# The second mixer of a two-block transformer on one NeuronCore: delta rule by pairs of heads beside the projections

## The chip, the cores and the metric

The kernel runs on one core of a Trainium2 chip. The metric is the device time in microseconds (us) of one execution, as the median of several runs. The trace is one further execution of the same program.

## The reference, cut to what matters

The program is two transformer blocks; all arithmetic is float32. The second block's first mixer works on 512 tokens: 256 of a context stream and 256 of a latent stream. Its input projection has parts `a_u`, `a_v` (a gated MLP), `qkv` and `gate` (a gated delta rule with 4 heads of 128, in both directions), and the decays and betas.

```python
def chunk_gmlp(u, v, ln_g, ln_b, ws, bs):
    u = gelu(u);  v = layer_norm(gelu(v), ln_g, ln_b)
    s = einsum('gij,bnjgd->bnigd', ws, chunks_of_128(v)) + bs
    return u * s

def gdn_chunked(q, k, v, g, beta, s0):        # per head, per chunk
    gcum = cumsum(g);  decay = exp(gcum_i - gcum_j) on and below the diagonal
    a_mat = strict_lower((k * beta) @ k.T * decay)
    t_mat = inverse(eye + a_mat)
    u = t_mat @ (v * beta);  w = t_mat @ (k * beta * exp(gcum))
    attn = (q @ k.T) * decay
    # over chunks, in order:
    v_new = u - w @ s
    o = (q * exp(gcum)) @ s + attn @ v_new
    s = s * exp(gcum_end) + (k * exp(gcum_end - gcum)).T @ v_new

def gated_deltanet(...):
    hq = silu(dwconv(qkv, conv_w));  q, k, v = split(hq);  q, k = l2norm(q), l2norm(k)
    o = forward scan + flipped backward scan
    return rms_norm(o, norm_g) * silu(gate)
y = concatenate([chunk_gmlp, gated_deltanet]) @ w_out
```

The context pass hands its final state to the latent pass. After `w_out` each stream gets a gated residual and a convolutional feed-forward.

## The kernel before, in words

All weights come as 547 tiles of 1 MB through a ring of 7 buffers (`load_turns`, line 166), in the order in which the program uses them; the host packs the stream in that order. `tile_used` counts used tiles and lets the next load start. A tile of a feature projection is 128 x 8 x 256: two halves of 128 features, each 8 products of 128x128 by 128x512, into one PSUM bank of 8 (`feature_tile`, line 198). One float32 product shows as two MATMUL records. `token_rows` (line 213) makes the rows of `v`: 2 tiles, 32 products in all.

Each engine runs its own instructions in program order. Semaphore counts (`Done`) order the engines. `after_all(eng)` makes an engine wait for all that the current chain has issued. `side_by_side` takes a list of generators and advances each by one `yield` in turn: one such turn is called a round here. It fixes the program order of every engine's queue; it doesn't look at times. TensorE needs no wait for its own earlier work.

The mixer has four stages.

1. `first_units` (line 1763) multiplies the first two tiles of the stream, which are those of `u`; `token_rows` follows with `v` in banks 0 to 3, then GELU on ScalarE.
2. `side_by_side` over three convolution lanes (`conv_lane`, line 1924; q, k and v, two of six tiles each, with products, taps, SiLU, square sums, root and transposes), a small lane (`gate_lane`: 2 tiles, w_ab; then `decay_steps`, `spatial_steps`), and `layer_norm_lane`.
3. A memset of the output sum on GpSimd (line 2135), and then `side_by_side` over four `delta_pair(d, pair)` chains: two directions by two pairs of heads. A chain has two PSUM banks of its own, starts `STAGGER * lane` rounds late (STAGGER is 5), and goes over 4 chunks of 128 tokens. A chunk has 35 yields: 7 for decays and triangular parts (ScalarE at 2182, TensorE at 2193 to 2196, VectorE at 2204, ScalarE at 2213, VectorE at 2223 to 2233, TensorE at 2241 and 2245), 20 for five levels of the inverse (TensorE 2281, ScalarE 2289, TensorE 2311 and 2314, VectorE 2322 to 2327), and 8 for the rest (TensorE 2337, 2352, 2369, 2385 to 2387, the others between). At 2213 stand the Exp functions.
4. The tail, in one stretch over all 16 head and tile pairs: squares on ScalarE (2415), power on GpSimd, scaling (2433), 16 transposes (2442), gating (2452). After it `modulation` (lines 996 and 997), and `out_stage`, whose products read the result `yT` (line 352) and whose gate diagonals are made at line 333.

```python
        def side_by_side(chains):
            before = {d: d.n for d in everyone}
            running = [(g, dict(before)) for g in chains]
            while running:
                for g, own in list(running):
                    chain.append(own)
                    if next(g, "end") == "end":
                        running.remove((g, own))
                    chain.pop()
```

Of the kernel before, what the change touches and what calls it, by code (L numbers as in the profile page):

```python
# [19 lines left out]
P = 128  # L20
# [43 lines left out]
def build(nc, stream, params, where, out):  # L64
# [4 lines left out]
    with ExitStack() as ctx:  # L69
# [245 lines left out]
        def out_stage(src, ktiles, ntt, x, outs_of, diag, gate=None, hidden_ready=None, kept=None, last_rows=None):  # L315
# [7 lines left out]
            if gate:  # L323
                layer, which, streams, rows, scr = gate
                groups = [(st, q) for st in streams for q in range(2)]
                gate_banks = range(4) if ntt == 4 else range(2)

                @block.vector
                def _(dve):
                    after_all(dve)  # L330
                    for n, (st, q) in enumerate(groups):
                        col = 24 * which + 16 + 4 * q
                        last = nc.vector.tensor_tensor(
                            scr[:, n, :].rearrange("p (a b) -> p a b", a=4), ident.unsqueeze(1).to_broadcast([P, 4, P]),
                            ada[:, layer, col:col + 4, st].unsqueeze(2).to_broadcast([P, 4, P]), ALU.mult)
                    dve_done.by(last)
                diag_known = dve_done.n

            def products(n, t, first):
                b = down[n][t]  # L340

                @block.tensor
                def _(pe):
                    claim(pe, b)
# [15 lines left out]
            def gate_rows_now():  # L360
                @block.tensor
                def _(pe):
                    pe.wait_ge(dve_done.sem, diag_known)
                    for n, b in zip(range(len(groups)), gate_banks):
                        claim(pe, b)
                        last = nc.tensor.matmul(ps[:, b, :], ones, scr[:, n, :], start=True, stop=True)  # L366
# [3 lines left out]
                def _(act):  # L370
                    act.wait_ge(pe_done.sem, pe_done.n)
# [5 lines left out]
            def add(n, t, summed, rows_known):  # L377
# [3 lines left out]
                def _(dve):  # L381
                    wait_marks(dve, [summed])
                    if gate:
                        dve.wait_ge(act_done.sem, rows_known)
                        st = streams[0] if ntt == 2 else (1, 1, 0, 0)[t]
                        link(dve, dve_done, nc.vector.tensor_tensor(scr[:, t, :], ps[:, b, :],  # L386
                                                                    rows[:, st, n * 512:n * 512 + 512], ALU.mult))
                        dve_done.by(nc.vector.tensor_tensor(xs, xs, scr[:, t, :], ALU.add))
# [1383 lines left out]
        def _(pe):  # L1772
            claim(pe, 4, 5, 6, 7)
            for n in range(2):
                t = tile_used.n + n
                pe.wait_ge(landed[t % RING], 16 * (t // RING + 1))
                first_units(pe, n, slice(0, SEQ))
# [20 lines left out]

        def gate_buffers():
            return take(2, D), take(4, 512)  # L1800

        reset(4 * 512)
# [4 lines left out]
        for i in range(4):  # L1807
            @block.scalar
            def _(act):
                act.wait_ge(tile_used.sem, tile_used.n - 1 + i // 2)  # L1810
                act_done.by(nc.scalar.activation(uT[:, i, :], ps[:, 4 + i, :], ACT.Gelu))
                freed[4 + i] = [(act_done, act_done.n)]
        token_rows([0, 1, 2, 3], hT, 0, KT)
        for t in range(T4):
            @block.scalar
            def _(act):
                act.wait_ge(tile_used.sem, tile_used.n)
                act_done.by(nc.scalar.activation(vn[:, t, :], ps[:, t, :], ACT.Gelu,
                                                 accum_out=small[:, 8 + t:9 + t]))
                freed[t] = [(act_done, act_done.n)]  # L1820

# [3 lines left out]
        mark_gdn = cur[0]  # L1825
        scratch512 = take(512)
        cbs = [take(2, 512) for _ in range(3)]
# [3 lines left out]
        def layer_norm_lane():  # L1831

            @block.vector
            def _(dve):
                after_all(dve)
                link(dve, dve_done, nc.vector.tensor_scalar(small[:, 12:16], small[:, 8:12], 1.0 / 512, None,
                                                            ALU.mult))
                for t in range(T4):
                    last = nc.vector.tensor_scalar(vn[:, t, :], vn[:, t, :], small[:, 12 + t:13 + t],
                                                   None, ALU.subtract)  # L1840
                dve_done.by(last)
# [3 lines left out]
            def _(act):  # L1845
                after_all(act)
                for t in range(T4):
                    link(act, act_done, nc.scalar.activation(scratch512, vn[:, t, :], ACT.Square,
                                                             accum_out=small[:, 8 + t:9 + t]))
            yield  # L1850
            rstd_of((8, 12), 512)
            yield

            @block.vector
            def _(dve):
                after_all(dve)
                for t in range(T4):
                    last = nc.vector.scalar_tensor_tensor(vn[:, t, :], vn[:, t, :], small[:, 24 + t:25 + t],
                                                          c("ln_g"), ALU.mult, ALU.mult)
                link(dve, dve_done, last)  # L1860
            yield

            @block.vector
            def _(dve):
                for t in range(T4):
                    last = nc.vector.tensor_tensor(vn[:, t, :], vn[:, t, :], c("ln_b"), ALU.add)
# [1269 lines left out]
```

## Time and profile before

| what | us |
|---|---|
| median of three runs | 3143.01 |
| lowest and highest run | 3138.71, 3143.89 |
| time of the profiled execution | 3139.56 |
| its span | 3137.6 |
| TensorE busy, of the span | 2915.2 (93%) |
| VectorE busy | 624.6 (20%) |
| ScalarE busy | 396.7 (13%) |
| mean granted TensorE clock | 0.960 |

The span runs from the first to the last instruction. The mixer lies between 1660 and 2160 us. TensorE's busy time there has to be read with the granted clock beside it, since a record takes twice as long on the lower level, and the record of a short matmul includes the time in which the next one has already begun.

### The profile page before, as it was taken

The page shows a single profiled execution, that of the slowest core. Times are in us where ns is not written, and L with a number is a line of the kernel's source. Part 1 is how long each engine was busy: PE and PEld are TensorE (multiplying, and loading weights), DVE is VectorE, ACT ScalarE, POOL GpSimd, SP SyncE. Part 2 cuts the span into 40 slices and gives each one's busy share as a digit, 9 for nine tenths or more (in the row PEclk, how much of TensorE's full clock was granted, in tenths as well). Part 3 has the DMA queues.
Part 4 walks back from the last instruction along what each step waited for, and adds up shares of the span by engine and source line. Part 5 has one row for each costly group of instructions (what it writes and reads, how often), then busy time and mean ns, then how long its engine had stood idle before and what let it go on. Part 6 is the DMA issues. An engine that isn't in the chain of part 4 may idle for free. (4 is left out here: it accounts for less than half of the span.)

```text
span 3137.6 us, 70498 instructions
## 1 busy us (share of the span) xinstructions
PE 2915.2 (93%) x31472; PEld 2178.4 (69%) x31472; DVE 624.6 (20%) x1701; ACT 396.7 (13%) x1066; POOL 32.7 (1%) x46
## 2 busy tenths in 40 slices
PE   5889999999999999999999996887999999889999
PEld 2567856679989899999996465774544444545883
DVE  0121001121100000001001135663222210223331
ACT  1110001110000000000001123332111100122210
POOL 0000000000000000000000000000000000000000
PEclk9899999999999999999999987888999999999999
DMA  8783434259989899999992110000112202311442
GB/s 346 303 333 134 149 146 147 106 213 347 365 339 369 337 369 351 365 364 358 357 385 91 67 41 15 2 2 25 70 67 81 81 27 81 134 67 54 144 151 80
DMA packets 80495, 585.60 MB, mean 187 GB/s; under 512 B 8912, under 2 KB 8912, under 8 KB 10064
## 3 DMA queue, kind: packets, MB, share of 16 engines
q1 hardware_dynamic: 79920, 580.15, 48.6%
q8 instruction: 251, 4.11, 0.5%
q10 hardware_dynamic: 288, 1.05, 0.1%
q14 instruction: 36, 0.29, 0.0%
HBM read 580.11 MB, written 1.05 MB: 185 GB/s over the span
## 5 line engine op out<-in xcount | busy, mean ns | idle before, releaser
L1448 PE MATMUL ps<-arena,ring 128*64 128x96 f32 x14336 | 601.9, 246 | 9.3 <-issue 8.1
L1448 PEld LDWEIGHTS ps<-arena,ring 128*64 128x64 f32 x14336 | 594.5, 137 | 20.3 <-issue 18.5
L2500 PE MATMUL ps<-hT,ring 128*128 128x256 f32 (+2 forms) x1472 | 455.3, 472 | 5.6 <-ACT hT L464 3.4
L2500 PEld LDWEIGHTS ps<-hT,ring 128*128 128x128 f32 x1472 | 274.5, 190 | 185.2 <-issue 166.3
L352 PE MATMUL ps<-ring,arena 128*128 128x512 f32 x896 | 388.3, 594 | 4.4 <-DVE small L996 4.4
L352 PEld LDWEIGHTS ps<-ring,arena 128*128 128x128 f32 x896 | 170.4, 191 | 216.4 <-issue 214.9
L1482 PE MATMUL ps<-arena,ring 128*64 128x96 f32 x7168 | 302.7, 246 | 10.2 <-issue 9.3
L1482 PEld LDWEIGHTS ps<-arena,ring 128*64 128x64 f32 x7168 | 297.8, 137 | 14.4 <-issue 13.4
L198 PE MATMUL ps<-hT,ring 128*128 128x256 f32 (+1 forms) x608 | 192.9, 478 | 8.2 <-ACT arena L749 4.0
L198 PEld LDWEIGHTS ps<-hT,ring 128*128 128x128 f32 x608 | 117.2, 194 | 81.8 <-issue 72.3
L1520 DVE TENSOR_TENSOR arena<-arena,ps 128x96 f32<-128x96 f32 x224 | 57.0, 255 | 574.2 <-ACT arena L1498 574.2
L1498 ACT ACTIVATE arena<-ps 128x96 f32<-128x96 f32 x224 | 56.3, 251 | 882.8 <-PE ps L1448 882.8
L923 PE MATMUL ps<-hT,ring 128*128 128x256 f32 (+1 forms) x736 | 152.7, 370 | 2.6 <-ACT hT L462 2.6
L923 PEld LDWEIGHTS ps<-hT,ring 128*128 128x128 f32 x736 | 134.8, 190 | 20.3 <-issue 3.0
L2545 DVE SCALAR_TENSOR_TENSOR arena<-ps,par,arena 128x510 f32<-128x510 f32 (+1 forms) x88 | 50.1, 611 | 300.6 <-ACT arena L2533 300.6
L213 PE MATMUL ps<-ring,hT 128*128 128x512 f32 (+1 forms) x224 | 96.5, 590 | 0.0
L568 PE MATMUL ps<-ring,arena 128*32 128x256 f32 x768 | 53.0, 437 | 35.9 <-DMA ring<-in_stream 35.9
L2533 ACT ACTIVATE arena<-ps,par 128x512 f32<-128x512 f32 (+1 forms) x88 | 46.3, 577 | 278.6 <-PE ps L2500 278.6
L213 PEld LDWEIGHTS ps<-ring,hT 128*128 128x128 f32 x224 | 43.2, 194 | 51.3 <-issue 47.1
L386 DVE TENSOR_TENSOR arena<-ps,arena 128x512 f32<-128x512 f32 x24 | 16.6, 692 | 261.2 <-PE ps L352 210.6
L1551 DVE COPY arena<-ps 128x384 f32<-128x384 f32 x16 | 8.9, 558 | 299.4 <-PE ps L1482 299.4
L568 PEld LDWEIGHTS ps<-ring,arena 128*32 128x32 f32 x768 | 28.5, 125 | 55.0 <-issue 44.2
(508 smaller groups left out, 2267.9 us busy)
## 6 DMA issues: line engine op xcount, KB each, us to landing
ring<-in_stream SPq DMA_DIRECT2D x547, 1024.0 KB, 6.0
par<-in_params SPq DMA_DIRECT2D x1, 3397.0 KB, 28.7
h<-in_x ACTq DMA_DIRECT2D x2, 512.0 KB, 7.8
cx<-in_ctx SPq DMA_DIRECT2D x2, 512.0 KB, 29.5
out<-h SPq DMA_DIRECT2D x4, 256.0 KB, 2.0
par<-in_params SPq DMA_DIRECT2D x1, 941.0 KB, 6.0
```

The source lines that it names most:

```text
L198: last = nc.tensor.matmul(o[:, 0:ntok], w[:, k, half * P:half * P + P], src[:, k, tok0:tok0 + ntok], start=(k == 0), stop=(k == KT - 1))
L213: last = nc.tensor.matmul(ps[:, b, 0:cols], src[:, k, tok0 + n * P:tok0 + n * P + P], w[:, k - t0, 0:cols], start=(k == 0), stop=(k == kti ...
L352: last = nc.tensor.matmul(ps[:, b, :], src[:, k, t * P:t * P + P], w[:, k % kper, :], start=(k == 0), stop=(k == ktiles - 1))
L568: last = nc.tensor.matmul(ps[32 * j:32 * j + 32, 7, 0:256], cond[:, k, :], w, start=(k == 0), stop=(k == KT - 1))
L923: last = nc.tensor.matmul(ps[:, b, half * SEQ + tok.start:half * SEQ + tok.stop], w[:, k, half * P:half * P + P], hT[:, k, tok], start=(k ...
L1448: last = nc.tensor.matmul(ps[m:m + 64, 4 + s % 2, half * P:half * P + CAP], w[:, k, half * P + m:half * P + m + 64], hTe[:, k, :], start=( ...
L1482: last = nc.tensor.matmul(ps[m:m + 64, 6 + half, q * P:q * P + CAP], w[:, j, q * P + m:q * P + m + 64], hid[:, 4 * d + j, :], start=(d == ...
L1498: nc.scalar.activation(sg[:, s % 2, :], ps[:, 4 + s % 2, 0:CAP], ACT.Silu).then_inc(moe_silu, 1)
L1520: nc.vector.tensor_tensor(hid[:, s, :], sg[:, s % 2, :], ps[:, 4 + s % 2, P:P + CAP], ALU.mult).then_inc(moe_hid, 1)
L2500: last = nc.tensor.matmul(ps[:, 2 * BANKS_CONV[f % RING] + half, tok], w[:, k, half * P:half * P + P], hT[:, k, tok], start=(k == 0), stop ...
L2533: nc.scalar.activation(buf[:, b, :], ps[:, 2 * b + half, 0:ntok], ACT.Copy, scale=tap(1, half, f)).then_inc(conv_centre, 1)
L2545: nc.vector.scalar_tensor_tensor(seg(o, 1, SEQ), seg(x, 0, SEQ - 1), tap(0, half, f), seg(o, 1, SEQ), ALU.mult, ALU.add).then_inc(conv_lef ...
```

## The change

The four stages become one `side_by_side` over decay lane, two delta lanes, projections, three convolution lanes, the MLP's rows and four tail quarters:

```diff
-        side_by_side([conv_lane(0), conv_lane(1), conv_lane(2), small_lane(), layer_norm_lane()])
-        side_by_side([delta_pair(d, pair) for d in range(2) for pair in range(2)])
+        side_by_side([decay_lane(), delta_lane(0), delta_lane(1), projections(),
+                      conv_lane((2, 3, 1), (4, 5), gT[:, 0:2, :]), conv_lane((4, 5), (6, 7), gT[:, 2:4, :]),
+                      conv_lane((0,), (0, 1), vn[:, 0:2, :]), mixed_rows(),
+                      *(tail_steps(pair, half) for pair in range(2) for half in range(2))])
```

`first_units` now takes tiles 2 and 4 of qkv (k and v of the first two heads). The stream order follows the order of use. `projections` issues the other products one by one:

```diff
+        def between(n):
+            for _ in range(2 if deltas else n % 2):
+                yield
+        def tile_products(kind, banks):
...
+            for half in range(2):
+                while banks[half] in busy:
+                    yield
+                for k in range(KT):
...                 # one product; weights(pe, kind) at the first
+                    if k < KT - 1 or half == 0:
+                        yield from between(k)
+        def value_rows():
+            while busy & {4, 5, 6, 7} or 0 not in conv_done:
+                yield
...                 # 2 halves x 4 row tiles x 4 products, each with: yield from between(k)
+        def projections():
+            used[0] = (yield from tile_products("qkv0", (0, 1)))[1][1]
+            for banks, n in (((3, 2), 0), ((6, 7), 2)):
+                halves = yield from tile_products("u", banks)
+                evacuated(halves, banks, [uT[:, n + i, :] for i in range(2)], ACT.Gelu)
+            for n, banks in ((3, (4, 5)), (5, (6, 7)), (1, (4, 5))):
+                used[n] = (yield from tile_products(f"qkv{n}", banks))[1][1]
+                yield
+            yield from value_rows()
+            while not {1, 3, 5} <= set(conv_done):
+                yield
+            for banks, n in (((4, 5), 0), ((6, 7), 2)):
+                halves = yield from tile_products("out_gate", banks)
+                evacuated(halves, banks, [gT[:, n + i, :] for i in range(2)], ACT.Silu, ...)
+            gates_of.extend(marks_here())
```

A delta lane takes one direction and does its two pairs of heads one after the other, 4 chunks of 35 yields each. The body of a chunk is that of before, except that the first chunk reads no state and the last writes none:

```diff
-        def delta_pair(d, pair):
-            for _ in range(STAGGER * lane):
-                yield
-            for T in ((0, 1, 2, 3), (1, 0, 3, 2))[d]:
+        def delta_lane(d):
+            for pair in range(2):
+                needed = (0, 2, 4) if pair == 0 else (1, 3, 5)
+                while not set(needed) <= set(conv_done) or not decays:
+                    yield
+                if pair == 0:
+                    while busy & {ba, bb}:
+                        yield
...
+                    for _ in range(STAGGER * d):
+                        yield
+                    deltas.append(d)
+                for step, T in enumerate(((0, 1, 2, 3), (1, 0, 3, 2))[d]):
...
+                    lane_marks[d, pair].append(marks_here())
+                    yield
```

`decay_lane` is `decay_steps` with the start of the small lane: 8 yields, in bank 2. `conv_lane(todo, bank, cb)` does `conv_steps(n, ...)` for each n once its tile is multiplied: 11 yields for k, 5 for v, 9 for q. `mixed_rows` is the layer norm and the spatial product; it starts when `values` is set and both lanes have ended pair 0. The convolution buffers lie in `gT` and `vn`, the output sum in a buffer of its own, and its memset stands before the `side_by_side`, as does `modulation`. The tail goes by pair and half of the tokens:

```diff
+        def tail_steps(pair, half):
+            while min(len(lane_marks[d, pair]) for d in range(2)) < 2 * half + 2 or not spatial or not gates_of:
+                yield
+            b = yield from some_bank()
...         # squares (4), yield; v and root, yield; scale, yield
+            if (pair, half) == (1, 1):
+                last_tail.append((b, turn_and_gate))
+                return
+            turn_and_gate()             # 4 transposes, 2 gating operations
+        def last_rows_of(t):
+            if t == 2:
+                last_tail[0][1]()
+            return others(spatial) + [m for pair in range(2) for m in tail_done[pair, t // 2]]
```

`out_stage` gets `rows_ready=last_rows_of`: the products of row tile t wait for the quarters of that half alone. The gate diagonals are made at the end of `mixed_rows` (`gates_known`), and the ScalarE copy of the gate rows waits for the lanes' end (`rows_free`).

## Rows read from the trace of the kernel before

**Rows 1.** Windows by stage: us, busy by engine, granted clock, DMA share, GB/s.
```profile
1702.70:1733.00 30.30, 27.60 (x65) 11.95 (x63) 0.05 (x1) 3.51 (x10) 0.00 (x0) 1.00 0.22 82
1733.00:1908.00 175.00, 161.01 (x480) 92.06 (x480) 46.55 (x83) 30.82 (x55) 9.77 (x8) 0.87 0.15 52
1908.00:2140.00 232.00, 186.67 (x2752) 169.47 (x2752) 149.68 (x576) 74.33 (x258) 1.75 (x7) 0.83 0.01 2
2140.00:2160.00 20.00, 3.45 (x17) 3.24 (x17) 5.74 (x11) 6.36 (x32) 2.90 (x1) 0.65 0.00 0
```
**Rows 2.** Timeline of TensorE: start, us, instruction; start and end of the mixer.
```profile
1702.67 27.63 PE L213 MATMUL ps<-ring,hT 128*128 128x512 f32 x64
2138.20 0.39 PE L2387 MATMUL ps<-par,hT 128*128 128x128 f32 x2
2159.85 8.62 PE L352 MATMUL ps<-ring,arena 128*128 128x512 f32 x16 [3.31 <-DVE small L996]
```
**Rows 3.** Waits of TensorE from 1908 to 2140: total us, times, longest.
```profile
PE ps L2241 <- issue: 26.8, 16, 5.7
```
**Rows 4.** Timeline of TensorE where records follow each other, at the full clock.
```profile
2105.74 0.28 PE L2311 MATMUL ps<-arena 64*64 64x64 f32 x4
2105.85 0.28 PE L2314 MATMUL ps<-arena 64*64 64x64 f32 x4
2137.75 0.39 PE L2385 MATMUL ps<-par,hT 128*128 128x128 f32 x2
2137.97 0.39 PE L2386 MATMUL ps<-par,hT 128*128 128x128 f32 x2
```
**Rows 5.** Windows of 5 us inside the delta stage.
```profile
2100.00:2105.00 5.00, 4.58 (x30) 4.14 (x29) 2.50 (x9) 2.33 (x8) 0.00 (x0) 0.66 0.01 3
2105.00:2110.00 5.00, 2.83 (x76) 2.50 (x77) 4.55 (x19) 1.48 (x6) 0.00 (x0) 1.00 0.00 0
```
**Rows 6.** Groups of TensorE, 1733 to 1908: busy us, mean ns, idle before.
```profile
L1980 PE MATMUL ps<-par,arena 128*128 128x1 f32 x64 | 14.0, 352 | 4.2 <-ACT arena L1969 4.2
L1892 PE MATMUL ps<-par,hT 128*128 128x16 f32 x64 | 12.5, 351 | 1.2 <-ACT arena L1882 1.2
L2034 PE MATMUL ps<-par,arena 128*128 128x128 f32 x32 | 5.6, 348 | 0.0
```
**Rows 7.** Timeline of one chunk's front from TensorE's 2196 to its 2241.
```profile
2105.16 0.61 DVE L2204 TENSOR_SCALAR par<-ps,arena 128x128 f32<-128x128 f32 x2 [0.64 <-PE ps L2196]
2106.18 0.42 ACT L2213 ACTIVATE par<-par 128x256 f32<-128x256 f32 x1
2107.58 0.42 DVE L2223 TENSOR_TENSOR hT<-ps,par 128x256 f32<-128x256 f32 x1
2109.52 0.29 DVE L2233 TENSOR_TENSOR par<-par,hT 128x128 f32<-128x128 f32 x1
2109.91 0.29 PE L2241 MATMUL ps<-par,hT 64*64 64x64 f32 x3 [1.62 <-issue]
```
**Rows 8.** Timeline of the last chain's end, nearly alone.
```profile
2132.24 0.41 PE L2337 MATMUL ps<-hT,par 64*64 64x64 f32 x4 [0.21 <-issue]
2139.32 0.42 DVE L2402 TENSOR_TENSOR arena<-arena,ps 128x256 f32<-128x256 f32 x1
```
**Rows 9.** Timeline of GpSimd and the table load of the delta stage.
```profile
1905.65 1.80 POOL L2135 MEMSET arena<- 128x2048 f32 x1 [8.95 <-DVE arena L2072]
1913.85 1.28 ACT L2213 ACT_TABLE_LOAD   x1 [4.85 <-DVE arena L2207]
```
**Rows 10.** Timeline of the tail's pieces.
```profile
2143.39 0.31 ACT L2415 ACTIVATE small<-arena 128x128 f32<-128x128 f32 x1
2147.45 2.90 POOL L222 TENSOR_TENSOR small<-small 128x16 f32<-128x16 f32 x1 [237.70 <-DVE small L2421]
2150.49 2.50 DVE L2433 TENSOR_TENSOR arena<-arena,small 128x512 f32<-128x512 f32 x4 [3.30 <-POOL small L222]
2156.64 2.73 DVE L2452 SCALAR_TENSOR_TENSOR arena<-ps,par,arena 128x512 f32<-128x512 f32 x4 [3.65 <-PE ps L2442]
```

More of the change, by code:

```diff
@@ L1773, in _ @@
             claim(pe, 4, 5, 6, 7)
-            for n in range(2):
+            for n, kind in enumerate(("qkv2", "qkv4")):
                 t = tile_used.n + n
+                order.append(kind)
                 pe.wait_ge(landed[t % RING], 16 * (t // RING + 1))
@@ L1797, in _ @@
                                                     float(D) ** 0.5, ALU.mult, ALU.mult))
+        next_mod = modulation(0, 1, c("norm2_0"))
         def gate_buffers():
-            return take(2, D), take(4, 512)
+            return take(2, D), [take(512) for _ in range(4)]
+        PAIR = 2
+        W = PAIR * P
         reset(4 * 512)
@@ L1806, in build @@
         gT = take(GH, 512)
[L1807 to L1820, printed above, removed]
+        osum = take(T4, GH * P)
         abv = take(T4, 16)
@@ new lines, in build, with _ @@
+        vecs = lambda x: x.unsqueeze(2).to_broadcast([P, PAIR, P])
+        heads = lambda x: x.rearrange("p (h n) -> p h n", h=PAIR)
+        both = lambda m: m.unsqueeze(1).to_broadcast([P, PAIR, P])
+        @block.gpsimd
+        def _(pool):
+            after_all(pool)
+            pool_done.by(nc.gpsimd.memset(osum, 0.0))
+        used = {2: tile_used.n - 1, 4: tile_used.n}
+        busy = {2, 4, 5, 6, 7}
+        conv_done, lane_marks, tail_done = {}, {(d, pair): [] for d in range(2) for pair in range(2)}, {}
@@ new lines, in build, with marks_here, others, adopt @@
+        decays, values, spatial, gates_of, gates_known, lanes_end, last_tail = [], [], [], [], [], [], []
+        deltas = []
+        def marks_here():
+            return [(d, n) for d, n in chain[-1].items() if n]
+        def others(marks):
+            return [(d, n) for d, n in marks if d not in (tile_used, pe_done)]
+        def adopt(*lists):
+            for marks in lists:
+                for d, n in marks:
+                    chain[-1][d] = max(chain[-1].get(d, 0), n)
+        def leave(*banks):
+            for b in banks:
+                freed[b] = others(marks_here())
+                busy.discard(b)
@@ new lines, in conv_steps, with _ @@
+                yield
+                @block.tensor
+                def _(pe):
+                    after_all(pe)
+                    for i in range(2):
+                        last = nc.tensor.matmul(ps[:, bank[i], :], ones, cb[:, i, :], start=True, stop=True)
+                    pe_done.by(last)
+                yield
+                @block.vector
+                def _(dve):
+                    after_all(dve)
+                    for i in range(2):
+                        last = nc.vector.scalar_tensor_tensor(
+                            full[i], full[i], float(P) ** -0.5 if kind == 0 else 1.0, ps[:, bank[i], :],
+                            ALU.mult, ALU.mult)
+                    dve_done.by(last)
@@ L2075, in decay_steps @@
-        def decay_steps():
             @block.tensor
@@ L2316, in _ @@
+                    yield
+                    @block.tensor
+                    def _(pe):
+                        after_all(pe)
+                        for n in range(PAIR):
+                            last = nc.tensor.matmul(ps[blocks2[src], bb, hc_of(n)], labc[blocks2[dst], hc_of(n)],
+                                                    heads(full)[blocks2[dst], n, blocks2[dst]], start=True, stop=True)
                         pe_done.by(last)
```

909 lines of the change are left out of this document (476 added, 433 removed).

## Prediction

> **What bounds the kernel now.** I read the windows by stage first. From the end of the first units, where the records of `v` begin, to the first product of the down projection it is 2159.85 - 1702.67 = 457.2 us [rows 2]; the change leaves what lies before and after as it is, so the sum is made over this stretch. DMA moves next to nothing in the delta stage (2 GB/s [rows 1]) and the ring is full then, so loads are not the limit. Three things cost time there. The 232 us of the delta stage have a granted clock of 0.83 and the VectorE is busy for 150 of them. The projections and convolutions take 175 us at a clock of 0.87. The tail has TensorE busy for 3.5 of 20 us. The busy column must not be trusted for work: 187 of 232 looks full, yet it is inflated by the lower clock and by the pipelined ends. So I price the work from starts of neighbouring records at the full clock.
>
> A 64x64 record follows the last after (2105.85 - 2105.74)/4 = 0.03 us, a 128x128 record after (2137.97 - 2137.75)/2 = 0.11 us [rows 4]. A chunk of one delta chain has 136 records of the first kind (8 at 2241, 24 in each of 5 levels, 8 after them) and 36 of the second (16, 4, 4, 12): 4.0 + 4.0 = 7.9 us. Sixteen chunks are 127 us of work in 232. Four chains in rounds with 15 of stagger are 4 x 35 + 15 = 155 rounds, so a round cost 1.50 us for 4 x 7.9/35 = 0.91 us of TensorE work. The waits show the largest hole: 26.8 us in 16 waits before line 2241 [rows 3]. It is a chain of three engines inside a chunk, from the end of 2196 over VectorE, Exp, and seven VectorE operations, 2105.0 to 2109.9 [rows 7], and TensorE's queue has nothing left that may overtake. A window with such a hole and the one before it have clocks of 1.00 and 0.66 [rows 5]: the lower level of 1.2 GHz comes in again and again after holes.
>
> **The change part by part.** First the order, from the yields. The projections issue two products per round until the first delta lane starts. qkv0 ends in round 8, and its convolution's 9 yields let lane 0 start in round 18; by then 34 products are issued. Lane 0 runs rounds 18 to 297, lane 1, five later, 23 to 302, since 8 chunks of 35 are 280. All projections are 8 feature tiles of 16 and 32 products for `v`, 160. The other 126 go at one per two rounds: u to 36, qkv3 to 66, qkv5 to 97, qkv1 to 128; then `value_rows` waits for the last convolution to round 138 and runs to 202, and the two gate tiles end in round 262. Pair 1 needs convolution 1, ready at 137, before round 158: no wait. `mixed_rows` runs from 202 to about 215. The first three quarters of the tail wait for the gates and run at 262; the last runs after 302. So there are three parts: 17 rounds without deltas, 245 with deltas and products, 40 with two delta lanes alone.
>
> A product is 27.63/32 = 0.86 us [rows 2].
>
> Part A, rounds 1 to 17. 34 products are 29 us. The w_ab product took 12.5 us at a mixed clock [rows 6]; between 6 and 12.5, I take 9. The tri product and the convolution steps of tiles 2, 4 and 0 (16 short records at 3.5 us by 14.0/4, half of it at the full clock; 16 transposing records of 0.11; 4 long ones of 0.43) are 13. The new start waits for `modulation` and then the memset of 1.8 us [rows 9], which was paid before too, ahead of the deltas: 3 us. Chain waits between ScalarE, VectorE and GpSimd that 1.7 us of products a round don't cover: 5, bounds 0 and 12. A = 59, between 53 and 68.
>
> Part B, 245 rounds, that is 7 turns of 35. Per turn: two chunks, 15.9 us; 18 products, 15.5 us; convolutions 3, 5, 1, the spatial products and the transposes of three quarters, 17 us in all by the records above, 2.4 a turn. That is 33.8 us of work, 0.97 a round against 0.91 before. The clock: before it was 0.83 with chains alone and 0.87 with products [rows 1]; I take 0.87, since each chunk still has its hole: 33.8/0.87 = 38.9. The hole before 2241 was 1.7 us a chunk (26.8/16). Behind it then stood six short operations of other chains; now stand three of the other lane and two products, about the same length, so I keep 1.7, 3.4 a turn. What remained before, 52.5 - 31.8/0.83 - 6.8 = 7.4 us a turn, I put on VectorE, which served four chains in queue order at 150/232 of the time; with two chains and products that don't depend on it I price this at nothing. The products hide it: between a level's short group and its next one, ScalarE or VectorE need less than 1 us, and 0.86 of product and a group of the other lane stand there. If that cover fails, it costs up to 7.4 x 7 = 52. ScalarE is new: Gelu, Silu and Exp now alternate. Exp comes at lane rounds 4 of a chunk, the others at 36, 68, 99, 130, 176, 184, 192, 200, 232 and 262; in order they make 17 table switches where the delta stage had one [rows 9]. At 1.28 us each that is 20 us of ScalarE more, of which I put half on the path, 1.4 a turn. Sum 43.7 a turn, 1.25 a round: B = 306. Bounds: at the full clock and with nothing lost 237; at the old 1.50 a round 367.
>
> The Trainium skill, "ScalarE: Activation LUTs", section "What ACT_TABLE_LOAD costs", says that a switch of set costs a drain beside the load, 2.66 us in all. The trace here has 1.28 for the load and shows no drain by itself. By the page the 17 switches would put another 11 us on the path by the same half, and the time would be 3099; my sum goes by the row. Its section "Rules for kernel authors" advises to do all of one set before switching; the change does the reverse.
>
> Part C, 40 rounds of two lanes alone. The last chain's final eight rounds took 2139.74 - 2132.24 = 7.5 us, 0.94 a round, with others still in the way at first [rows 8]. The operations alone of one chunk (7.9 of TensorE, 74.3/16 = 4.6 of ScalarE, 149.7/16 = 9.4 of VectorE [rows 1], and some 35 handovers of 0.1 us, the estimate from 2105.0 to 2105.16 between 2196 and 2204 [rows 7]) are 25 us, 0.72 a round. I take 0.9: C = 36, between 29 and 44.
>
> Part D, the end. Before, from the last delta product to the down projection it was 21.7 us (2138.20 to 2159.85) [rows 2]. Now the first two row tiles of the down projection wait for quarters done in round 262, so products start at once, and `modulation` and the gate diagonals are behind. The last quarter needs 4 squares (6.4/16 = 0.4 each [rows 1, 10]), a quarter of the power's work (under 2.9), and a quarter of the scaling's 2.5 [rows 10]: 5 us beside 14 us of products; its 4 transposes (0.9) and its quarter of the gating's 2.7 [rows 10] stand in TensorE's queue ahead of tile 2, 2 to 3 us. D = 3. The ScalarE copy of the gate rows waits for the lanes' end, some 1 us after TensorE, covered too.
>
> What is removed for good is small: 8 state products of first chunks and as many state updates, under 4 us, left in as margin. The order of the stream changes no amount; ten tiles of 1 MB over some 400 us instead of some 205 ask less of the ring. The SyncE queue only waits for `tile_used`, which now grows evenly.
>
> Sum: 59 + 306 + 36 + 3 = 404 against 457.2, 53 less. The profiled execution took 3139.6 (span 3137.6 and 2.0 around it), so 3086.5; its time is 3.5 below the median of 3143.01, whose 53 less is 3090. I take 3088.
>
> **The rivals.** First, TensorE-bound: with a product always ready the holes shrink below what drops the clock. Then B goes towards 260 (1.06 a round) and A to 55: 55 + 260 + 32 + 3 = 350, 107 less, 3034. For it speaks that the windows with products and no chain waits, 1702 to 1733, had a clock of 1.00 [rows 1]. Against it: queue order is kept, so a product behind a waiting 2241 doesn't run, and a chunk has this hole as before.
>
> Second, slower: rounds stay at 1.5 us. The mechanism is the fixed order of the queues. With two lanes each must take 8 chunks in sequence, 285 rounds where 155 sufficed, and if a round's length is set by engines handing over and not by the amount in it, the doubled number of rounds eats all that the overlap gives. Its place is part B and C: 245 x 1.5 + 40 x 1.1 + 62 + 4 = 478, 21 more, 3162. It decides from (457.2 - 62)/285 = 1.39 us a round. For it: TensorE's work in a round is as large as before (0.97 to 0.91), and the old round took 1.50. Against it: VectorE has half the chains in a round, and the lane's bare latency is 0.72.
>
> Third, it doesn't do what it says in the tail: three quarters wait for the gates anyway, and if the chains end before the projections instead of 40 rounds after them, the quarters stand open at the end: 16 squares at 0.4 and what follows, about 12 us, 3100 with the rest as above. By the counts of yields this is unlikely.
>
> **How the numbers follow.** Less than 0.2%, 6 us, can't be told from no change here. Forecast (B at 1.1 to 1.37 a round, 3048 to 3125): 0.66. TensorE-bound, 3000 to 3048: 0.20. Tail open, inside the forecast's range: 0.05. Slower or nearly even, over 3137: 0.09. Range for eight in ten: 3038 to 3128, which leaves out a strong form of the first rival and the second. Faster 0.90, within 0.2% 0.02, slower 0.08.
>
> **What would show it.** Line 2241's successor still waits near 1.7 us a chunk (right) or under 0.5 (first rival). The mean granted clock of the stretch is 0.85 to 0.92 (right), over 0.95 (first rival). The stretch with products beside the chains is some 300 us, that with chains alone some 36, ending in the down projection within 2 us of the last chain's product. About 17 table loads stand in it. It would be wrong if a round of part B takes under 1.1 or over 1.39 us, if a chunk of a lane takes over 48 us, or if pair 1 of a lane starts later than the end of pair 0.

## The result, and the profile after

The changed kernel takes 3168.55 us in the median of four runs (3159.6 to 3174.8), the kernel before 3140.86 beside it. The ratio is 1.0087, 95% interval [1.0059, 1.0116]: 27 us slower. I had forecast 3088. The profiled execution is the shortest of the four: 3159.6, against the 3139.6 of before.

The stretch of the sum, from the end of the first units to the down projection, took 2168.15 - 1696.7 = 471.5 us; it was 457.2 [rows 2] and forecast at 404 (with 3 us for the end, which by this border now fall behind it). Windows of the three parts, in the columns of [rows 1]:

```profile
1696.70:1757.50 60.80, 57.22 (x209) 35.38 (x209) 18.72 (x39) 19.26 (x30) 5.64 (x5) 0.86 0.15 52
1757.50:2114.00 356.50, 296.59 (x2689) 183.65 (x2687) 159.81 (x537) 103.02 (x276) 4.28 (x3) 0.90 0.06 22
2114.00:2168.00 54.00, 38.66 (x365) 34.24 (x365) 23.99 (x86) 15.30 (x59) 3.29 (x3) 0.63 0.06 21
```

Part A came out at 61 (forecast 59). Part B, 245 rounds with products, took 356 and not 306: 1.46 us a round. Part C, 40 rounds of two lanes alone, took 54 and not 36: 1.35 a round, at a clock of 0.63. Borders of the parts, TensorE's timeline:

```profile
1682.65 14.05 PE L1774 MATMUL ps<-hT,ring 128*128 128x256 f32 x64 [1.69 <-ACT hT L1764]
1699.71 11.91 PE L2091 MATMUL ps<-par,hT 128*128 128x16 f32 x64 [3.01 <-POOL arena L1841]
...
2113.00 1.13 PE L1891 MATMUL ps<-hT,ring 128*128 128x512 f32 x2
...
2167.72 0.64 PE L2480 MATMUL ps<-par,arena 128*128 128x128 f32 x2
2168.15 7.67 PE L358 MATMUL ps<-ring,arena 128*128 128x512 f32 x16
...
2188.61 29.40 PE L358 MATMUL ps<-ring,arena 128*128 128x512 f32 x64 [2.06 <-DVE arena L2563]
```

The wait for the memset is 3.0 us, the down projection starts right behind the last chain product, and the last quarter costs 0.6 of transposes and 2.1 of waiting: all as forecast. [rows 3] shows the largest wait of before. TensorE now has several (whole stretch; the last line is from the kernel before, 1908 to 2140):

```profile
PE ps L2332 <- issue: 27.1, 13, 4.0
PE ps L2372 <- ACT par L2361: 12.0, 7, 3.6
PE ps L2402 <- issue: 10.5, 7, 5.1
PE ps L2284 <- ACT arena L2274: 8.4, 5, 5.1
```
```profile
PE ps L2193 <- ACT arena L2183: 7.4, 4, 5.5
```

L2332 is the 2241 of before: 2.1 us each time, and the same total. L2284, the chunk's first products, is the 2193 of before and waited about as much there. Larger than before are the waits of the levels, 2372 and 2402. The 2372 that waits here is the first of a chunk's levels: its lane's four scaled copies (2361) stand just ahead of it in the lane's chain, and `after_all` makes it wait for them, although the product doesn't read them. The table loads from 1757.5 to 2168 were counted right, 17, where [rows 9] had one:

```profile
L2304 ACT ACT_TABLE_LOAD x9 | 11.5, 1283 | 5.3 <-PE ps L1891 4.8
L1905 ACT ACT_TABLE_LOAD x3 | 3.8, 1283 | 0.3 <-ACT par L2436 0.3
L1990 ACT ACT_TABLE_LOAD x3 | 3.8, 1283 | 5.7 <-DVE arena L1982 5.6
L1935 ACT ACT_TABLE_LOAD x2 | 2.6, 1283 | 6.3 <-PE ps L1924 6.3
```

Of the 20 us between the two profiled executions the stretch holds 14. Another 12 lie behind it: 3.5 in the down projection, and most of the others in code that the change doesn't touch, at a lower clock, such as the attention's score products (before, then after); what lies ahead was 6 us shorter. That part is chance: the two-lane kernel below has the same code behind the stretch as the kernel before, and took 986.6 us for it where the kernel before took 977.8 and the changed one 989.7. So I go by the ratios from here, and set beside them the stretch of the profiled execution, which leaves this out.

```profile
L2840 PE MATMUL ps<-hT,arena 128*128 128x512 f32 x32 | 18.7, 668 | 1.4 <-issue 1.4
L2842 PE MATMUL ps<-arena 64*128 64x512 f32 x32 | 18.0, 641 | 0.0
```
```profile
L2967 PE MATMUL ps<-hT,arena 128*128 128x512 f32 x32 | 22.6, 796 | 1.4 <-issue 1.4
L2969 PE MATMUL ps<-arena 64*128 64x512 f32 x32 | 21.8, 765 | 0.0
```

### The profile page after: what moved, and what is told of

It is laid out like the page before. It is cut to its first block and busy times, and to the rows that moved or that the text cites. A ratio compares the mean times of both kernels' runs of the same rounds, so it can differ in the third digit from the quotient of the medians.

```text
span 3157.8 us, 70495 instructions
## 1 busy us (share of the span) xinstructions
PE 2931.7 (93%) x31424; PEld 2153.7 (68%) x31424; DVE 624.4 (20%) x1692; ACT 418.3 (13%) x1082; POOL 32.5 (1%) x43
## 5 line engine op out<-in xcount | busy, mean ns | idle before, releaser
L2627 PEld LDWEIGHTS ps<-hT,ring 128*128 128x128 f32 x1472 | 274.5, 190 | 185.2 <-issue 166.3
L930 PE MATMUL ps<-hT,ring 128*128 128x256 f32 (+1 forms) x736 | 152.7, 370 | 2.6 <-ACT hT L469 2.6
L930 PEld LDWEIGHTS ps<-hT,ring 128*128 128x128 f32 x736 | 134.8, 190 | 20.3 <-issue 3.0
L1891 PE MATMUL ps<-hT,ring 128*128 128x512 f32 x256 | 144.9, 673 | 0.0
L198 PE MATMUL ps<-hT,ring 128*128 128x256 f32 x352 | 80.3, 389 | 4.0 <-ACT arena L756 4.0
L198 PEld LDWEIGHTS ps<-hT,ring 128*128 128x128 f32 x352 | 68.1, 195 | 15.5 <-issue 6.1
L213 PE MATMUL ps<-ring,hT 128*128 128x512 f32 (+1 forms) x160 | 68.7, 589 | 0.0
```

Source lines behind the costliest of these rows:

```text
L198: last = nc.tensor.matmul(o[:, 0:ntok], w[:, k, half * P:half * P + P], src[:, k, tok0:tok0 + ntok], start=(k == 0), stop=(k == KT - 1))
L213: last = nc.tensor.matmul(ps[:, b, 0:cols], src[:, k, tok0 + n * P:tok0 + n * P + P], w[:, k - t0, 0:cols], start=(k == 0), stop=(k == kti ...
L930: last = nc.tensor.matmul(ps[:, b, half * SEQ + tok.start:half * SEQ + tok.stop], w[:, k, half * P:half * P + P], hT[:, k, tok], start=(k ...
L1891: last = nc.tensor.matmul(ps[:, banks[half], :], w[:, k, half * P:half * P + P], hT[:, k, :], start=(k == 0), stop=(k == KT - 1))
L2627: last = nc.tensor.matmul(ps[:, 2 * BANKS_CONV[f % RING] + half, tok], w[:, k, half * P:half * P + P], hT[:, k, tok], start=(k == 0), stop ...
```

## The experiments

Twelve kernels ran. All are compared with the kernel before on the same chip (3131 to 3137 us there); a difference in us is the difference of ratios times 3137. The last column is the stretch from the end of the first units to the down projection in the profiled execution.

| kernel | ratio to before | 95% interval | us against before | stretch, us |
|---|---|---|---|---|
| before | 1 | | 0 | 457 |
| changed | 1.0087 | 1.0059 to 1.0116 | +27 | 472 |
| products by pairs | 1.0155 | 1.0130 to 1.0181 | +49 | 492 |
| 90 products left out | 1.0066 | 1.0042 to 1.0089 | +21 | 466 |
| one table | 1.0028 | 1.0016 to 1.0040 | +9 | 454 |
| products in the holes | 1.0191 | 1.0169 to 1.0213 | +60 | 503 |
| before, two lanes | 1.0369 | 1.0342 to 1.0396 | +116 | 570 |
| before, two lanes, products | 1.0408 | 1.0390 to 1.0427 | +128 | 573 |
| changed, lanes 17 apart | 1.0174 | 1.0152 to 1.0196 | +55 | 509 |
| changed, lanes 1 apart | 1.0058 | 1.0041 to 1.0074 | +18 | 459 |
| before, tail by halves | 0.9975 | 0.9958 to 0.9992 | -8 | 436 |
| new front, four chains, 5 apart | 0.9934 | 0.9912 to 0.9956 | -21 | 438 |
| the same, 9 apart | 1.0065 | 1.0041 to 1.0089 | +20 | 470 |
| the same, 1 apart | 0.9917 | 0.9892 to 0.9941 | -26 | 422 |

**Is TensorE's queue full?** The first suspicion from the trace: a product that stands alone between groups of 64x64 is followed by a gap. One level of both lanes with two products of 0.86:

```profile
2096.51 0.33 PE L2402 MATMUL ps<-arena 64*64 64x64 f32 x4
...
2097.59 1.12 PE L1891 MATMUL ps<-hT,ring 128*128 128x512 f32 x2
2098.64 0.68 PE L2372 MATMUL ps<-arena 64*64 64x64 f32 x16
2099.26 1.13 PE L1891 MATMUL ps<-hT,ring 128*128 128x512 f32 x2
2100.31 0.33 PE L2402 MATMUL ps<-arena 64*64 64x64 f32 x4
```

Four rounds took 3.80 us for 3.1 of work, so about 0.17 us would go at each change between product and short group, an estimate from these rows. A round takes 0.95 us here, far under the mean of 1.46. First test, half as many changes:

```diff
-            for _ in range(2 if deltas else n % 2):
+            for _ in range((4 if deltas else 1) * (n % 2)):
                 yield
```

> The same work in the same order, but beside the delta lanes the products go by two in every four rounds, not by one in every two. Theory A (each product that stands alone between short 64x64 groups costs TensorE two handovers of some 0.17 us, 43 us over 126 products): 63 pairs of handovers go, about 20 us less than the changed kernel: 3140 to 3152. Theory B (a round's length is set by the chain's handovers between the engines, whatever stands in it): no change, 3160 to 3175, or a little slower because two of four hops have no cover.

It became 21 us slower than the changed kernel. Theory A's gain did not show; whatever the changes cost, it is outweighed. That every second hop now has no cover is the reason I give, argued and not shown. The next run leaves out products:

```diff
-                        last = nc.tensor.matmul(ps[:, banks[half], :], w[:, k, ...], hT[:, k, :], ...)
+                        if k in (0, KT - 1) or not deltas:
+                            last = nc.tensor.matmul(ps[:, banks[half], :], w[:, k, ...], hT[:, k, :], ...)
```

(and the same for the rows of `v`)

> The changed kernel without 90 of the 126 projection products that stand beside the delta lanes (the first and last of each accumulation stay, so all waits and the order stay); it leaves out that part of the projections. Those 90 are 77 us of TensorE at the full clock. Theory A (TensorE's queue is full beside the lanes: its work and handovers set the round): 77 us and some 30 us of handovers go, 3060 to 3095. Theory B (the chains set it and the products lie in their gaps): under 30 us less, 3140 or more.

77 us of TensorE work are gone and 7 us of time. Theory A falls: the 107 us it promised are not there, so TensorE's queue was not the limit at the clock of the changed kernel. The window of the parts B and C of this kernel (1759.5 to the down projection) says what else happened:

```profile
1759.50:2165.50 406.00, 287.19 (x2876) 222.27 (x2875) 184.95 (x624) 118.84 (x335) 7.57 (x6) 0.74 0.06 22
```

The same 406 us, and the granted clock is 0.74 where the changed kernel has 0.90 and 0.63. How much time would have gone at an unchanged clock, this run doesn't say.

**Can the products be put where the hole is?** A counter `pos[d]` of a lane's yields was added:

```diff
-            for _ in range(2 if deltas else n % 2):
-                yield
+            spent[0] += 1
+            while spent[0] >= max(QUOTA.get(pos[d], 0) for d in range(2)):   # {2: 3, 3: 3, 4: 3, -1: 2}
+                yield
+                spent[0] = 0
```

> The same work, but beside the lanes the products are issued three in each of the three rounds after a lane's yields 2, 3 and 4 (the hole ahead of the first 64x64 group of a chunk), and none in the other rounds: 18 in 35 rounds as before. Theory A with C (C: the uncovered hole of each chunk, with the lower clock after it, is the other large part): handovers between sizes fall to 6 groups in 35 rounds and the holes are filled, 35 to 50 us less than the changed kernel, 3118 to 3133, and the waits ahead of that first group nearly vanish. Theory B: the rounds keep their length and some get three products on top, 3165 or more.

33 us slower than the changed kernel. Program order is the reason I give, argued and not shown: three products ahead of the other lane's step hold that lane up by 2.6 us a round. The clock is a rival: from 1764 to 2200 it was granted 0.77, where parts B and C of the changed kernel have 0.86 together.

**What do two lanes cost by themselves?** The decisive run, one part of the change alone:

```diff
-            for _ in range(STAGGER * lane):
+            for _ in range(STAGGER * d if pair == 0 else 0):
...
-        side_by_side([delta_pair(d, pair) for d in range(2) for pair in range(2)])
+        def in_sequence(d):
+            yield from delta_pair(d, 0)
+            yield from delta_pair(d, 1)
+        side_by_side([in_sequence(d) for d in range(2)])
```

> The kernel before with one part of the change alone: the four delta chains of its delta stage run on two lanes, each direction one pair after the other, with nothing beside them; 285 rounds where there were 155 in 232 us. Theory B (a round costs the same 1.35 to 1.5 us whether two chains or four stand in it): the stage takes 385 to 425 us, 3285 to 3330. The prediction's idea (the fewer chains in a round, the shorter it is, down to 0.7 to 0.95 us): 205 to 270 us, 3105 to 3180.

116 us slower. The delta stage takes 345 us for the 285 rounds, 1.21 a round, where four chains took 232 for 155. Both numbers of the expectation are missed: a round did get shorter with fewer chains (1.50 to 1.21), but by a fifth and not by half. Then products were added to this, and the two lanes got two pairs of banks so that the other four are free for them:

```diff
-            ba, bb = 2 * lane, 2 * lane + 1
+            ba, bb = 4 * d, 4 * d + 1
...
+        def other_products():
+            for n in range(140):
+                @block.tensor
+                def _(pe):
+                    nc.tensor.matmul(ps[:, (2, 3, 6, 7)[n % 4], :], ident, gT[:, n % 4, :], start=True, stop=True)
+                yield
+                yield
+        side_by_side([*(in_sequence(d) for d in range(2)), other_products()])
```

> The two-lane run again (delta chains on two lanes, nothing of the front moved), with 140 more products of 128x128 by 128x512 put beside the lanes, one per two rounds, whose results nobody reads: 120 us of TensorE at the full clock, without the convolution lanes and table loads of the changed kernel. The stage took 345 us with two lanes alone at a granted clock of 0.67. Theory P (the products lie mostly in the lanes' gaps, and what they cost comes partly back by the clock they hold up): clock 0.88 or more, the stage 360 to 390 us, 15 to 45 us more than the two-lane run. Theory Q (each product pushes the lanes back by its own length): 450 us or more.

The delta stage, without and with 120 us of products:

```profile
1901.00:2246.00 345.00, 250.50 (x2751) 219.32 (x2752) 153.82 (x573) 77.11 (x257) 2.51 (x9) 0.67 0.01 1
```
```profile
1901.00:2248.00 347.00, 307.71 (x3030) 191.50 (x3030) 152.47 (x573) 76.32 (x257) 1.84 (x7) 0.97 0.01 2
```

The stage is 2 us longer, the run 12 by the ratios (the intervals allow 2 to 22). Theory P holds, beyond its numbers. The products ask 120 us of TensorE and the clock goes from 0.67 to 0.97; what they cost and what the clock gives back are equal to the eye, and these runs don't part the two. What the chain of one lane waits for is seen in the two-lane run's timeline. Lane 1's state products end; lane 0's front stands ahead on VectorE:

```profile
1995.29 0.39 PE L2387 MATMUL ps<-arena 128*128 128x128 f32 x2
1995.38 0.42 DVE L2223 TENSOR_TENSOR arena<-ps,arena 128x256 f32<-128x256 f32 x1 [1.45 <-ACT arena L2215]
...
1997.41 0.29 DVE L2233 TENSOR_TENSOR arena<-par,arena 128x128 f32<-128x128 f32 x1
1997.62 0.60 DVE L2396 SCALAR_TENSOR_TENSOR arena<-arena,ps 128x128 f32<-128x128 f32 x2
...
1998.87 0.41 ACT L2182 ACTIVATE arena<-arena 128x256 f32<-128x256 f32 x1 [3.67 <-DVE arena L2402]
1999.64 0.80 PE L2193 MATMUL ps<-par,arena 128*128 128x128 f32 x2 [0.75 <-ACT arena L2183]
```

The products end at about 1995.7, and until 1997.62 nothing of lane 1 moves, although its input is ready: VectorE works through lane 0's front first.

The mean of 1.21 us hides two kinds of rounds. While both lanes are in the levels of the inverse, each four rounds of the two-lane run take 3.44 us, 0.86 a round:

```profile
1970.18 0.69 PE L2281 MATMUL ps<-arena 64*64 64x64 f32 x8 [0.26 <-issue]
...
1973.62 0.69 PE L2281 MATMUL ps<-arena 64*64 64x64 f32 x8 [0.26 <-issue]
...
1977.05 0.69 PE L2281 MATMUL ps<-arena 64*64 64x64 f32 x8 [0.26 <-issue]
```

With two products in them they take 3.80, in the last run as in the changed kernel. A chunk of 35 rounds has 15 in which both lanes are in their levels, so by an estimate from these rows they take 13 of the 42 us, and the 20 rounds in which one lane is in its front or at its end take 29, about 1.5 each. The halved number of chains did make the level rounds short, as the prediction had it; it did not shorten the fronts.

**The table loads.**

```diff
-                    act_done.by(nc.scalar.activation(dst, ps[:, b, :], func))
+                    act_done.by(nc.scalar.activation(dst, ps[:, b, :], ACT.Copy))
```

(Square for the Gelu of `v`, Copy for the Silu of tiles 1, 3, 5)

> The changed kernel with Gelu and Silu beside the delta lanes replaced by Copy or Square (it leaves those functions out), so that Exp's table stays loaded from the lanes' start: some 16 of the 17 table loads of 1.28 us go, the activations stay. If a table load stops a lane's chain each time (theory B, chains set the time): 15 to 25 us less than the changed kernel. If the lanes' other waits cover them: under 5 us less. The prediction had put half of them, 10 us, on the path.

One load is left in parts B and C:

```profile
L2304 ACT ACT_TABLE_LOAD x1 | 1.3, 1283 | 4.8 <-PE ps L1891 4.8
```

It saves 18.5 us, 1.16 us for each of 16 loads, and the stretch is 17 us shorter, 1.07 each. Both say that most of a load's 1.28 us stands on the path, but the difference of the two ratios allows some 9 to 28 us, so the half that was forecast, 10, is not excluded. The Trainium skill, "ScalarE: Activation LUTs", section "What ACT_TABLE_LOAD costs", would have them at 2.66 us with a drain, an estimate of 43 us in all. Both measurements stand against the page here.

**How far apart should lanes stand?** `STAGGER = 17` in the changed kernel:

> The changed kernel with the second lane 17 rounds behind the first and not 5, half a chunk, so that one lane's long front lies beside the other's levels. It adds 12 rounds at the end. If the holes add up because both lanes' fronts follow each other closely, the stretch gets shorter by more than the 12 rounds cost (16 us): 10 to 30 us less in all. If every round has its price whatever meets in it: 12 to 17 us more.

27 us slower by the ratios and 38 in the stretch, 10 to 20 more than 12 empty rounds explain; neither side of the expectation came true. With `STAGGER = 1`:

> The changed kernel with the second lane 1 round behind the first and not 5 (17 cost it some 27 us). Theory M: two fronts of a chunk meet in the same rounds and are paid once, in 8 chunks, 4 rounds fewer: 15 to 35 us less than the changed kernel, 3120 to 3145, at or under the kernel before. Rival (a front is paid by its own length on VectorE and ScalarE, whether two meet or not): within 6 us of the changed kernel.

9 us faster by the ratios, where the intervals reach to nothing, and 13 in the stretch: in the direction of theory M but under its range, and over the rival's.

**Which parts of the change are worth having?** The tail alone, on the old kernel: after the second chunk of all four chains the first 256 tokens are squared and scaled, turned once lanes 0 and 1 have ended; the second half goes beside the first products.

```diff
-        side_by_side([delta_pair(d, pair) for d in range(2) for pair in range(2)])
+        side_by_side([delta_pair(d, pair) for d in range(2) for pair in range(2)] + [first_half()])
...
+        def last_rows_of(t):
+            if t == 1:
+                turn and gate the second half
+            return [half_done[t // 2]]
```

> The kernel before with one part of the change alone: four chains and separate stages as before, but the tail by halves of the tokens, the first half beside the last chunks, the second beside the first products of the down projection; modulation and gate diagonals earlier. If the tail's 21.7 us are really off the path with it and nothing else changes: 17 to 21 us less than the kernel before, 3120 to 3125. If they come back as a wait of the down projection or as a later start of the chains: under 8 us less, 3133 or more.

By the ratios 8 us of the 17 to 21, and the interval of 3 to 13 us excludes the expected size. But the stretch of the profiled execution is 436.5 us, 21 shorter, which is the expected size. What lies behind the stretch took 987.0 us there and 977.8 in the kernel before, 9 longer, as in most other kernels of the table; the profiled kernel before had the shortest of all. So the tail did leave the path, and the rest of the difference lies outside this stretch; its cause stays open. Then the changed front before the four chains, one product pair a round and no lanes in it:

```diff
-        side_by_side([decay_lane(), delta_lane(0), delta_lane(1), projections(), ...])
+        side_by_side([decay_lane(), projections(), conv_lane(...), conv_lane(...), conv_lane(...), mixed_rows()])
+        side_by_side([delta_pair(d, pair) for d in range(2) for pair in range(2)] + [first_half()])
```

> Not two lanes: the changed kernel's front (units of qkv2 and qkv4 first, projections by two products a round, convolution lanes, decays and the MLP's rows side by side) without delta lanes in it, then the four chains of the kernel before, with the tail by halves as in the run with halves. If the products beside the convolution chains keep TensorE full: the 205 us from the first units to the chains become 180 to 192, and with the tail 3100 to 3115 where before is 3135. If the old front was as good: as the run with halves alone, 8 us under before.

3117.9 us in the median, 21 us under the kernel before. But the front did not do what was expected: from the end of the first units to the chains' first product it took 213.5 us, not 180 to 192, where the kernel before took 206.

```profile
1686.32 15.49 PE L1774 MATMUL ps<-hT,ring 128*128 128x256 f32 x64 [1.69 <-ACT hT L1764]
1915.28 0.49 PE L2284 MATMUL ps<-par,arena 128*128 128x128 f32 x2 [2.28 <-ACT arena L2274]
```

The whole stretch is 438 us, as with the halves alone. So the 13 us by which its ratio is better than theirs can't be put down to the front. Its chains 9 and 1 rounds apart:

> The version with the changed front, four chains and the tail by halves, with the chains 9 rounds apart (a quarter of a chunk) and not 5. It adds 12 rounds, partly empty. If four fronts of a chunk that lie close together are what TensorE waits for: 5 to 15 us less than the same version with 5. If the empty rounds cost more than that: 5 to 12 us more.

> The version with the changed front, four chains and the tail by halves, with the chains 1 round apart and not 5: still on four different steps of a level, but the fronts of their chunks meet in nearly the same rounds, and there are 12 rounds fewer. Theory M (a round costs what the longest step in it costs, so fronts that meet are paid once and fronts that are spread are paid each): 15 to 40 us less than the same version with 5, the reverse of what 9 did (41 us more). Rival (with all four fronts together VectorE's 2.5 us per front adds up and TensorE has nothing meanwhile): 5 us less to 20 us more.

The chain stages of the three, for 1 (143 rounds), 5 (155) and 9 (167):

```profile
1909.00:2117.00 208.00, 175.81 (x2758) 161.36 (x2759) 150.81 (x581) 78.01 (x272) 2.59 (x5) 0.83 0.02 6
```
```profile
1915.30:2139.30 224.00, 176.64 (x2760) 158.74 (x2761) 150.85 (x580) 76.93 (x271) 2.32 (x4) 0.90 0.02 6
```
```profile
1918.70:2175.40 256.70, 194.05 (x2760) 171.99 (x2761) 152.59 (x580) 75.93 (x271) 2.30 (x4) 0.84 0.02 5
```

1.45, 1.45 and 1.54 us a round: the same work in more rounds takes longer by at least the rounds' price. By the runs 9 costs 41 us against 5, both sides of its expectation missed; 1 gains 5, within the intervals' reach of nothing, though its stage and its stretch are 16 shorter. The version with 1 has the best ratio of all, 0.9917, in the median 3108 us, and a stretch 35 us shorter than the kernel before: by the stretches 21 of it came with the tail by halves and 16 with the small stagger.

## Why the prediction was wrong

The order of the rounds, part A, the absence of a wait for pair 1, the number of table loads, the wait before 2241's successor, the end: right. Part B took 356.5/7 = 50.9 us a turn of 35 rounds where the sum had 43.7, and part C 54 where it had 36.

The failed step is this sentence: the remainder of "7.4 us a turn, I put on VectorE ...; with two chains and products that don't depend on it I price this at nothing". VectorE and ScalarE still serve everything in queue order, and the price came out at 7.2 us a turn, nearly what the prediction named for the case that the cover fails. Three terms hold it.

First, the lanes themselves. The two-lane run with products, which has no convolutions and no table loads in it, takes 347/285 = 1.22 us a round, 42.6 a turn. For this much the sum had 43.7 less 1.4 of loads and 2.8 of convolutions, 39.5: short by 3.1. Part C has the same fault: 40 rounds of two lanes alone at the measured 1.21 are 48, not 36. I had summed the bare chunk, 25 us, from durations at the full clock, while the lanes alone have 0.67 and a chunk of 35 rounds takes 42, and had let each lane run as if the other's front did not stand in the same three queues. So the 285 rounds cost 345 us before anything is put beside them, a little more than the 306 + 36 that were forecast with everything beside them, where 155 rounds of four chains cost 232. This alone is +116 by the runs.

Second, what else stands beside the lanes. The sum priced the convolutions, the MLP's rows and the tail's quarters by their TensorE work alone, 2.8 us a turn, and their VectorE and ScalarE work at nothing. The turns of lane 0, from one chunk's first 64x64 group (2332, or 2241) to the next, show what it cost:

| turn | beside the lanes, by the trace | changed, us | two lanes, products, us |
|---|---|---|---|
| 1 | GELU of `u` | 44.8 | 44.0 |
| 2 | convolution 3 | 54.2 | 41.5 |
| 3 | convolution 5 | 48.8 | 43.7 |
| 4 | convolution 1 | 53.1 | 41.9 |
| 5 | GELU of `v` | 46.7 | 45.6 |
| 6 | last GELU, the MLP's rows, first SiLU of the gates | 62.0 | 41.2 |
| 7 | second SiLU of the gates, three quarters | 52.2 | 42.1 |

Turn 7 reaches 15 us into part C. The excess of 62 us lies almost wholly in turns 2, 3, 4, 6 and 7. In turn 6 the MLP's rows and the gate diagonals have 15 us of VectorE work, and a lane's step waits behind one such group although its product is done:

```profile
2040.25 2.49 DVE L2191 TENSOR_TENSOR arena<-arena,par 128x512 f32<-128x512 f32 x4
2040.80 0.31 PE L2405 MATMUL ps<-par 64*64 64x64 f32 x4
2042.65 0.28 DVE L2413 TENSOR_TENSOR arena<-arena,ps 128x128 f32<-128x128 f32 x1
```

Less some 2.5 a turn for the loads, 5.8 a turn remain for these lanes, 3.0 more than in the sum. This is read from the traces; no run took them away. In part C, 5.1 us go in one wait of 2284 while ScalarE squares the three quarters.

Third, the table loads: 2.4 to 2.6 us a turn for 1.4, short by about 1.1, with the uncertainty named above.

On the clock the forecast held in size: 0.86 over the stretch and 0.90 in part B, for 0.87. Its reason for the lower level, holes, is not the whole of it: from 1966.9 to 1981.6 in the two-lane run TensorE waits never longer than 0.4 us and is granted 0.50 throughout. The first rival wanted over 0.95 for the stretch and did not get it. It is true that products hold the clock up (0.67 to 0.97 beside two lanes), but they saved nothing beyond their own cost.

The second rival came nearest: the doubled rounds eat the overlap, and its 3162 was 7 from the result. I gave it 0.09. That is in part luck. Its 1.5 us a round stood for a round set by handovers and not by what is in it; the runs have 0.86 to 0.95 in the levels, 1.21 in the mean of two lanes alone, and the rest up to 1.46 is the work of the other lanes and the loads. What I held against it, that VectorE has half the chains in a round, is true and was worth 0.29 us in the mean.

The balance against the kernel before: two lanes +116, table loads +18.5, the tail -8 (measured on four chains), sum +126.5; measured is +27. So moving the other projections beside the lanes brought 99 us, nearly the 126 x 0.86 = 108 of their length: the overlap worked. By the stretches it is 113 + 17 - 21 = 109 against 14, so 95. This last is the remainder of the balance, not a run of its own. Part B and C together hold 410.5 - 345 - 18.5 = 47 us more than the two-lane rate and the loads explain; the table above shows in which turns.

## What to carry to other kernels

When chains of dependent short steps are laid side by side in fixed program order, count rounds first and price a round from a measured one; fewer chains do not make a round proportionally shorter (half the chains took a fifth off it here), so keep as many chains abreast as the banks allow. Price what is put beside the chains by its time on every engine whose queue the chains use, not by TensorE alone. Long independent products beside two such chains were nearly free here, yet only worth it if they don't force the chains into sequence. Activations with another table in a chain's ScalarE queue cost it most of a load each.

## What the runs showed of the hardware

TensorE ran 120 us of additional products beside two lanes in a stage that grew from 345 to 347 us, with the granted clock going from 0.67 to 0.97; and 77 us of products could be left out for 7 us of time, with the clock falling to 0.74. Short 64x64 groups that follow each other with waits of at most 0.4 us were granted the lower level, 1.2 GHz, for 15 us on end:

```profile
1966.90:1981.60 14.70, 12.96 (x196) 11.51 (x194) 6.53 (x26) 2.50 (x9) 0.00 (x0) 0.50 0.01 2
```

With a 128x512 product in every second round, the same part of a chunk was granted 1.00 (1958 to 1975 of the run with products). A change between a 128x512 product and a group of 64x64 took about 0.17 us in the level shown above, an estimate from its rows.
